# In the V stage of a retention and expert-retrieval block, GpSimd's low half waits for the weighing of its place, and four of nine gathers follow the last of a group

## What is computed

```
ue  = take(u, idx)                              # rows of u for the 128 chosen experts of a token
act = gelu(einsum('td,ted->te', x, ue))
out = einsum('te,ted->td', gate * act, take(v, idx))
h   = h + out
```

## Time and profile before

| | |
|---|---|
| median of 3 executions | 3949.08 us (3942.32 to 3951.86) |
| the profiled execution | 3940.36 us, its span 3938.3 us |
| mean granted TensorE clock | 0.949 of full speed |
| busy share of the span | PE 89%, POOL 61%, DVE 72%, ACT 26% |
| V stage | about 2660 to 3780 us from the span's start |
| busy in 3000 to 3200 us | PE 91%, DVE 84%, POOL 58%, ACT 20% |
| DMA in that stretch | 0.85 of the engines' time, 284 GB/s |

### The profile page before, as it was taken

The page is one execution under the profiler, slowest core; times in us unless marked ns, Lnnn a source line. Parts: engine busy times, 40 slices in busy tenths (PEclk is TensorE's granted clock), DMA queues, the critical chain, the costliest instruction groups (busy, mean ns, idle before and its releaser), DMA issues.

```text
span 3938.3 us, 59196 instructions
## 1 busy us (share of the span) xinstructions
PE 3514.5 (89%) x22379; PEld 3412.9 (87%) x22379; DVE 2827.3 (72%) x4151; ACT 1008.0 (26%) x1654; POOL 2409.5 (61%) x1612
## 2 busy tenths in 40 slices
PE   7899888878989889999999999997889989988877
PEld 6799788777989889988989899997888888888765
DVE  5524477866555654999999999635888888878854
ACT  2310221121000121144545455302222222212132
POOL 5488563325678776876766668865555555555522
PEclk9999899888999999999999999998999999999988
DMA  4244421114666767877878777877888888888811
GB/s 143 77 123 123 128 87 56 45 39 146 217 223 235 249 224 265 297 277 273 285 274 307 277 288 277 314 259 247 277 285 287 282 282 284 287 269 283 276 38 59
DMA packets 324293, 852.82 MB, mean 217 GB/s; under 512 B 27552, under 2 KB 125344, under 8 KB 320672
## 3 DMA queue, kind: packets, MB, share of 16 engines
q0 software_dynamic: 110592, 402.70, 28.0%
q1 hardware_dynamic: 72864, 258.15, 21.6%
q10 hardware_dynamic: 140672, 189.82, 13.8%
HBM read 755.67 MB, written 94.90 MB: 216 GB/s over the span
## 4 chain that ended last, share of the span: by engine, by line
PE 37%; DVE 12%; DMA 5%; POOL 3%; issue 3%; ACT 2%; ACTq 1%; DVEq 0%; POOLq 0%; SPq 0%
PE main L630 26%; PE main L869 7%; DVE h L1853 5%; DMA rows<-v_rows,s_idx 5%; DVE scr L1529 4%; PE scr L828 4%; POOL v_lo L595 2%; ACTq L1207 1%; ACT v_hi L1217 1%; DVE rows L1522 1%; DVE res L1864 1%; POOL rows L568 1%; POOL w_lo L541 0%; PE scr L728 0%; DVE hot L1787 0%
## 5 line engine op out<-in xcount | busy, mean ns | idle before, releaser
L541 POOL TENSOR_TENSOR w_lo<-raw,w_hi 128x1024 fp32r<-128x1024 f32 x346 | 873.2, 2524 | 27.9
L539 POOL CAST w_hi<-raw 128x1024 fp32r<-128x1024 f32 x346 | 367.8, 1063 | 677.5 <-issue 428.6
L630 PE MATMUL main<-mix_hi,w_hi 128*128 128x320 f32 (+1 forms) x2816 | 691.1, 320 | 84.1 <-POOL w_lo L541 44.1
L630 PE MATMUL main<-mix_lo,w_hi 128*128 128x320 f32 (+1 forms) x2816 | 677.9, 315 | 0.0
L630 PE MATMUL main<-mix_hi,w_lo 128*128 128x320 f32 (+1 forms) x2816 | 676.9, 315 | 0.0
L1529 DVE SCALAR_TENSOR_TENSOR scr<-rows,s_dot,scr 128x1024 f32<-128x1024 f32 x381 | 489.1, 1284 | 230.8 <-DMA rows<-v_rows,s_idx 219.0
L869 PE MATMUL main<-h_hi,v_hi 128*128 128x320 f32 x2048 | 490.5, 322 | 120.4 <-DVE res L1864 101.8
L630 PEld LDWEIGHTS main<-mix_hi,w_hi 128*128 128x128 f32 x2816 | 480.7, 191 | 91.5 <-issue 61.6
L568 POOL DMA_INDIRECT rows<-u_rows,s_idx x384 | 405.4, 1056 | 238.1 <-DVE s_dot L1522 134.2
L595 POOL TENSOR_TENSOR v_lo<-raw,v_hi 128x1024 fp32r<-128x1024 f32 x128 | 308.0, 2407 | 389.3 <-ACT v_hi L1217 378.1
L630 PE MATMUL main<-a_hi,w_hi 128*128 128x320 f32 (+1 forms) x1728 | 477.4, 331 | 70.3 <-POOL w_lo L541 43.8
(11 more groups left out here) (231 smaller groups left out, 4967.1 us busy)
## 6 DMA issues: line engine op xcount, KB each, us to landing
raw<-stream SPq DMA_DIRECT2D x474, 512.0 KB
act_d<-actb ACTq DMA_DIRECT2D x128, 320.0 KB
gate_d<-gbuf ACTq DMA_DIRECT2D x20, 2048.0 KB
h<-act_d ACTq DMA_DIRECT2D x128, 320.0 KB, 4.9
gate_in<-gate_d ACTq DMA_DIRECT2D x31, 1280.0 KB, 13.4
rows<-u_rows,s_idx POOLq DMA_INDIRECT x384
rows<-v_rows,s_idx POOLq DMA_INDIRECT x384, 5.8
score_d<-stage ACTq DMA_DIRECT2D x16, 320.0 KB
```

Source lines behind the costliest of these rows:

```text
L539: pool.tensor_copy(w_hi[:, s, :], raw[:, s, :]).then_inc(hi_made, 1)
L541: pool.tensor_tensor(w_lo[:, s, :], raw[:, s, :], w_hi[:, s, :].bitcast(F32), ALU.subtract) \
L630: last = pe.matmul(main[s][:, dst:dst + n], wt[:, s, c * P:(c + 1) * P], rows[:, c, src:src + n], start=(c == 0 and wt is w_hi and rows is ...
```

## The change

POOL's loop over the blocks of the V stage gets a wait for `h32_ready`, so that the low half of block n is made only after DVE has weighed place n; and the nine gathers of a group are issued as 1, 2, 2 and 4 behind places 0 to 3, where they were 2, 2, 2 and 3. No instruction that computes or moves data is added or removed.

```diff
--- before.py
+++ after.py
@@ -591,11 +591,12 @@
             pool.wait_ge(tile_done, 2 * B_PAIR)
             for n in range(NE):
+                pool.wait_ge(h32_ready, n + 1)
                 pool.wait_ge(v_hi_made, n + 1)
                 pool.tensor_tensor(v_lo[n // EG % 2][:, n % EG, :], raw[:, n % 2, :],
                                    v_hi[n // EG % 2][:, n % EG, :].bitcast(F32), ALU.subtract).then_inc(v_split, 1)
                 if n >= EG:
-                    for _ in range(3 if n % EG == EG - 1 else 2):
+                    for _ in range((1, 2, 2, 4)[n % EG]):
                         if at_row[0] < DOTS:
                             gather()
             while at_row[0] < DOTS:
```

## The result

The changed kernel takes **4445.86 us** (median of 4, 4442.09 to 4447.36) against 3947.32 us of the kernel before (4 executions beside it): a ratio of 1.126, 95% interval 1.124 to 1.128. The forecast was 4345 us with a range of 4255 to 4435. The sign was forecast, and the path too (gathers that go out just ahead of their dots); the size was too small by a fifth (+ 499 us against + 398), and the time lies above the range.

A forecast was written before the change was run, and what follows sets the result against it. It took DVE's order in the V stage as the bound: a group of 44.75 us with stalls plus 1.5 for the clock, less 33.3, over 31 groups gives + 401 us, stated as 4345 us; range 4255 to 4435.

The forecast's parts named there:

- What bounds the kernel: V stage: DVE's order is the bound, 32.8 us counted of a 33.3 us group; PE needs 29.3 us.
- The pairing of gathers and dots: V stage: each gather is issued just ahead of its own dot, so three new stalls a group, at dots 0, 1 and 3.
- The stalls at dots 0 and 1: DVE, behind the weighings of places 0 and 1: L + 2.81 us each, 8.1 us.
- L: Time from a gather's issue on POOL to its dot on DVE: taken as 5.3 us, between 4.8 and 5.8.
- The stall at dot 3: DVE, behind the weighing of place 3: L + 0.55 us, with the remaining collision inside it.
- Dots 4 to 8: DVE, rest of a group: their gathers go out early enough, so no stall.
- The clock: PE in the V stage: slow spells after idling add 1.5 us a group, with 0 and 3.4 as the ends.
- the end of the sum with two spells: PE's clock in the V stage: upper end, two slow spells a group showing, 3.4 us.
- The prediction's own sign of being wrong: V stage: stalls present but a group over 3.4 us longer than 28.85 + 3 L would mean the clock step was too small.
- 28.85 + 3 L: Length in us of a new V-stage group on DVE with its three stalls, before the clock's part: 44.75 us.
- the second-bound rival: PE becomes the second bound, two slow spells and tiles at 3.7 us: 49.65 us a group, 4455 us; chance 0.12.
- the port is what counts: Rival: low halves no longer collide with weighings, the group falls to PE's pace, some 29.8 us: 3840 us; chance 0.03.

The follow-up runs named there:

- lead4_plain: The kernel before plus one extra gather behind each of the V stage's first four low halves (a stock of four), nothing else: 3876.64 us, ratio 0.983.
- wait_only: The kernel before with the wait for h32_ready alone, gathers still as 2, 2, 2, 3: 4150.21 us, ratio 1.051.
- free0: The changed kernel with the wait taken off place 0 alone, places 1 to 3 keeping it: 4376.46 us, ratio 1.108.
- gates_late: The changed kernel with the load of the next gates held back until drain 4 is done: 4341.88 us, ratio 1.099.
- lead4_5004: The kernel before with a stock of four gathers, the wait on places 1 to 3 only, and gathers as 5, 0, 0, 4: 3791.31 us, ratio 0.961.
- lead4_wait: The kernel before with the wait on all places, the old order 2, 2, 2, 3 and a stock of four gathers: 3932.84 us, ratio 0.996.
- lead4_both: The changed kernel (wait, and order 1, 2, 2, 4) with a stock of four gathers: 3930.56 us, ratio 0.996.

## Why the prediction was right and wrong

**What bounds the kernel** was read rightly: DVE's order, with gathers issued just ahead of their dots. lead4_plain confirms it from the other side; four gathers in stock, with no other edit, gave 70 us.

**The pairing of gathers and dots** was right: stalls at dots 0, 1 and 3, none at 2. wait_only moved the stalls to the dots that the same count names, and free0 shortened the one at the dot that it names.

**The stalls at dots 0 and 1**, forecast 8.1 us each, measured 7.7 and 7.8 from the start of the unhindered dot (means of 30 groups): L is 5.0 and 5.1, not 5.3. Errors of - 0.4 and - 0.3.

**The stall at dot 3 is the step that failed.** It was L + 0.55 = 5.85 with the same L as the others. Measured: dot 3 starts at 3231.86, unhindered it would at 3219.85 + 2.66 = 3222.51; 9.35 us in this group, 8.4 to 10.5 in all, 9.25 in the mean. L for gather 3 is 9.2 in the mean, not 5.3. What lay under it: the prediction listed the raw load and the activations' load among what moves, and forgot **the load of the next gates**. ScalarE issues it behind the cast that follows weighing 3. In the changed kernel weighing 3 comes 2.7 us behind weighing 2, so the load starts beside gather 3 at the moment when DVE waits for just that gather.

The price was to be had before any run. In the kernel before, gather 6 goes out 0.6 us ahead of the gates' load (POOL, ScalarE's queue, DVE):

```profile
3183.94 1.36 POOL L568 DMA_INDIRECT rows<-v_rows,s_idx  x1 [0.16 <-issue]
```

```profile
3184.51 0.38 ACTq L1210 DMA_DIRECT2D gate_in<-gate_d  x1
```

```profile
3192.82 1.29 DVE L1529 SCALAR_TENSOR_TENSOR scr<-rows,s_dot,scr 128x1024 f32<-128x1024 f32 x1 [0.38 <-DMA rows<-v_rows,s_idx]
```

From issue to dot, 8.9 us; 8.8 to 10.3 in the 26 groups in which dot 6 waited for it. Because DVE had other dots in hand, only 0 to 1.8 us of that showed as a wait. The landing times that L was taken from, 7.4 at most, don't contain these times from issue to dot, so they were no upper bound for L. gates_late took 104 us off, 3.4 a group, as much as the whole gap between forecast (4345) and result (4446), and brought dot 3's stall to 5.65 us, where 5.85 was forecast.

**Dots 4 to 8** were to wait for nothing; 0.35 us a group was measured, mostly at dot 4.

**The clock.** Forecast 1.5 us a group; DVE's waits for PE, without the start of the stage and the group with the pause (7.2 us), are (76.5 - 18.7 - 7.2) / 29 = 1.7. The stretches show the pattern, PE at rest and then the lower of its two levels (1.2 instead of 2.4 GHz) for most of 4 us, in the changed kernel:

```profile
3230.00:3234.00 4.00, 0.07 (x1) 0.07 (x1) 2.14 (x3) 0.00 (x0) 1.88 (x2) 0.56 1.03 376
3234.00:3238.00 4.00, 4.00 (x17) 4.00 (x18) 3.37 (x5) 0.00 (x0) 0.00 (x0) 0.59 1.04 399
3238.00:3242.00 4.00, 4.00 (x30) 4.00 (x29) 3.93 (x4) 0.00 (x0) 0.00 (x0) 1.00 0.34 128
```

The Trainium skill's rule (TensorE: Matmul & The Clock Gate, HAM oscillation) that a matmul stream broken by waits falls back to half rate agrees in kind: the mean clock of 3000 to 3200 us fell from 0.97 to 0.85. But only 1.7 us a group reached DVE, so the end of the sum with two spells, 3.4 us, didn't come about. The prediction's own sign of being wrong pointed here all the same: a group is 49.8 - 44.75 = 5 us longer than 28.85 + 3 L with L = 5.3, over the 3.4 that were to mean that the step on PE's clock was too small. It was L. The extra time beyond the forecast was not PE's, though the second-bound rival (4455 us) names the right time for the wrong reason.

**The sum again**, with the measured terms: 22.7 + 7.7 + 7.8 + 9.25 (with place 3's collision in it) + 0.35 + 1.7 = 49.5 of 49.8 us.

**A slip in the sum** that changes nothing here: 4341 + 8.7 is 4350, not the 4345 that was stated. The result lies above the range by either.

**The rivals.** That the port is what counts was false for this change: the collisions fell from 2.04 to 0.94 us a weighing, a gain of 4.4 us a group, and the gathers took 18.3 (DVE's wait for them, (728.8 + 7.8) / 31 = 23.8 us against (162.9 + 5.3) / 31 = 5.4). Something like it came true in lead4_5004, where PE's pace decides. The range was too narrow above, because L had one value for all three gathers, with a spread of 4.8 to 5.8.

What stays open: lead4_wait and lead4_both differ by 2 us though their collisions differ (mean weighing 2.17 against 1.85 us, waits for the activations 62 against 98 us); that these two cancel was read from the table above, not tested. That the activations' loads come late because gathers and gates go out just ahead of them was read from the stretches, too, and no run moved them alone. Loading the activations a group earlier wasn't tried, since the low halves of h are written over their buffer, and PE still reads them.

## What to carry to other kernels

Before an engine is told to wait, list what stands behind the wait in its queue and how soon each of these is needed: here the low half could wait, but the gathers behind it could not. Lay such transfers in first, a few places ahead. That alone does not make the wait pay: with four gathers in stock, the wait on all four places still cost 56 us in the old order and, on places 1 to 3, was worth 41 us in the order 5, 0, 0, 4; without the stock it cost 201. And when a change moves one instruction of a chain, follow every DMA that hangs on it to its new neighbours: the gates' load was nearly harmless where DVE had other rows in hand, and took the time of a gather from 5 to 9 us where the kernel was waiting for just that gather. Look for the price in the old trace first, from issue to use, and not in a median.

## What was unexpected of the hardware

The gates' load of 1280 KB took 13.4 us from issue to landing in the kernel before and 17.8 us in the changed one, although the DMA engines' mean share in the stage fell from 0.85 to 0.55. In the changed kernel they stand nearly still for some us (0.09 in 3150 to 3154) and are full (0.98 to 1.04) in 3226 to 3238, while gathers 3 to 8, raw blocks and the gates are under way together. The mean share of the stage said nothing about the latency of one transfer in it; the 4 us slices did. A gather of 512 KB took 5 us from issue to its dot with the queues quiet, and 9 us there.
